# Dense U and V blocks of a group in one transfer each, and sparse phases of 19, 17, 17 and 11 groups

## The reference

```python
# per block of 128 tokens: eb = the 8 x 16 chosen experts of each token, gb = their gates
h = jnp.einsum('td,ted->te', xb, u[eb])          # u, v: (16384, 1024)
a = jax.nn.gelu(h, approximate=False) * gb
y = jnp.einsum('te,ted->td', a, v[eb])
# afterwards: h = layer_norm(alpha * h + y)
```

## Time and profile before

| | |
|---|---|
| median of 3 runs | 3060.47 us (3056.7 to 3060.66) |
| the profiled execution | 3062.79 us |
| its span, first to last instruction | 3061.1 us |
| mean granted TensorE clock | 0.938 |
| TensorE busy | 85% of the span |
| VectorE busy | 75% |
| GpSimd busy | 53% |
| ScalarE busy | 34% |
| moved by DMA | 833 MB |

### The profile page before, as it was taken

The page is one execution under the profiler, slowest core; times in us unless marked ns, Lnnn a source line. Parts: engine busy times, 40 slices in busy tenths (PEclk is TensorE's granted clock), DMA queues, the critical chain, the costliest instruction groups (busy, mean ns, idle before and its releaser), DMA issues.

```text
span 3061.1 us, 40460 instructions
## 1 busy us (share of the span) xinstructions
PE 2617.2 (85%) x14808; PEld 2033.3 (66%) x14808; DVE 2307.9 (75%) x4894; ACT 1049.6 (34%) x1649; POOL 1620.0 (53%) x1187
## 2 busy tenths in 40 slices
PE   7998788889996565644678999999999999999996
PEld 5886676778775565542445767777767777677775
DVE  4512667657999899965777778777778777789999
ACT  4412334333544676751112222322222322222322
POOL 0010011024887555545666666677666767766774
PEclk9999899999998787876889999999999999999999
DMA  4323222131111799999999999999999999999995
GB/s 129 127 81 118 85 87 87 45 119 52 58 59 36 260 300 309 322 296 373 379 383 387 391 386 382 401 394 397 387 394 376 408 404 409 391 382 347 366 377 209
DMA packets 309808, 833.44 MB, mean 272 GB/s; under 512 B 26128, under 2 KB 114640, under 8 KB 309616
## 3 DMA queue, kind: packets, MB, share of 16 engines
q0 software_dynamic: 150864, 548.60, 46.7%
q1 hardware_dynamic: 158752, 282.31, 26.1%
HBM read 771.93 MB, written 58.88 MB: 271 GB/s over the span
## 4 chain that ended last, share of the span: by engine, by line
PE 18%; DVE 12%; DMA 12%; POOL 8%; issue 5%; ACT 0%; SPq 0%; DVEq 0%; ACTq 0%; POOLq 0%
DMA e_u_row<-in_u,ids 11%; POOL hold L2081 5%; DVE e_u_row L2319 3%; PE psum L2157 3%; PE psum L2124 3%; PE psum L2158 3%; PE psum L2159 3%; PE psum L2125 3%; PE psum L2126 2%; PE psum L2172 2%; POOL e_u_row L2072 2%; DVE e_y L2309 2%; DVE e_u_row L2328 1%; DVE e_vl L2277 1%; DVE hold L2328 1%
## 5 line engine op out<-in xcount | busy, mean ns | idle before, releaser
L2072 POOL DMA_INDIRECT e_u_row<-in_u,ids x384 | 485.6, 1265 | 330.3 <-DVE ids L2319 236.3
L2319 DVE CUSTOM_DVE_ANT_0 e_u_row<-e_u_row,hold 128x1024 f32<-128x1024 f32 x384 | 468.3, 1224 | 242.6 <-DMA e_u_row<-in_u,ids 242.0
L2157 PE MATMUL psum<-e_vh,e_ah 128*128 128x512 f32 x1024 | 420.7, 411 | 102.1 <-DVE e_y L2309 82.6
L2081 POOL DMA_INDIRECT hold<-in_v,ids x376 | 435.5, 1158 | 134.4 <-issue 108.8
L2158 PE MATMUL psum<-e_vl,e_ah 128*128 128x512 f32 x1024 | 409.2, 400 | 0.0
L2159 PE MATMUL psum<-e_vh,e_al 128*128 128x512 f32 x1024 | 407.4, 398 | 0.0
L2124 PE MATMUL psum<-x1d,e_uh 128*128 128x512 f32 x864 | 341.0, 395 | 0.0
L2125 PE MATMUL psum<-x1d,e_uh 128*128 128x512 f32 x864 | 337.2, 390 | 0.0
L2157 PEld LDWEIGHTS psum<-e_vh,e_ah 128*128 128x128 f32 x1024 | 198.1, 193 | 209.2 <-DVE e_y L2309 109.9
L2126 PE MATMUL psum<-x1d,e_ul 128*128 128x512 f32 x864 | 336.3, 389 | 0.0
L2309 DVE TENSOR_TENSOR e_y<-e_y,psum 128x512 f32<-128x512 f32 x464 | 299.7, 681 | 13.1 <-PE psum L2159 13.1
(11 more groups left out here) (407 smaller groups left out, 5628.9 us busy)
## 6 DMA issues: line engine op xcount, KB each, us to landing
e_vr<-in_v SPq DMA_DIRECT2D x128, 512.0 KB, 6.7
e_ur<-in_uT SPq DMA_DIRECT2D x108, 512.0 KB, 7.2
s_G<-g_tile SPq DMA_DIRECT2D x8, 4096.0 KB, 27.0
e_g<-s_G SPq DMA_DIRECT2D x64, 512.0 KB, 9.0
ids<-in_w_ch SPq DMA_DIRECT2D x17, 512.0 KB, 4.1
s_ch<-p_out POOLq DMA_DIRECT2D x16, 512.0 KB, 3.3
hold<-in_wq SPq DMA_DIRECT2D x16, 512.0 KB, 4.4
hold<-in_v,ids POOLq DMA_INDIRECT x476, 8.7
```

The costliest lines, as they stand in the source:

```text
L2072: pool.indirect_dma_start(out=u_ring[n % U_RING][:], out_offset=None, in_=io["u"], in_offset=bass.IndirectOffsetOnAxis(ap=id_u[:, s, k:k + ...
L2081: pool.indirect_dma_start(out=v_ring[m % V_RING], out_offset=None, in_=io["v"], in_offset=bass.IndirectOffsetOnAxis(ap=id_v[:, t:t + 1], a ...
L2157: nc.tensor.matmul(acc, ah[s][j][:, r], vh[s][j][:, c], start=(first and j == 0), stop=False)
L2319: nc.vector.tensor_tensor_reduce(row, row, xs[:, s, :], 1.0, 0.0, ALU.mult, ALU.add, hs[:, s, k:k + 1]).then_inc(dotted, 1)
```

## The change

- `PHASE` becomes (0, 19, 36, 53, 64): the first phase has 19 groups, the second 17; the third and the last stay at 17 and 11.
- The arrays in HBM are laid out by groups. `uT` has both blocks of a group side by side in each partition's row, and V has a second copy `v2` in the same manner (the old `v` stays, for the gathers). So both blocks are one transfer of 1 MB whose runs are 8 KB. U blocks loaded singly (before the experts, and the first dense group's) take their 4 KB out of the 8 KB rows (`u_block`).
- The raw V blocks have no tile of their own: `v_raw[s]` is declared and released, so that `v_low[s]` gets its addresses; the subtraction then writes the low part over the raw data. The V load of g waits until TensorE is done with values(g-2), whose low part stands there, and no longer for the splits.
- The U load of g+1 waits for both splits of g.
- ScalarE splits V after both halves of the rest of its list. VectorE's split of V block 0 moves from ahead of weigh 1 to behind the last dot, just ahead of adds 6 and 7.

```diff
--- before.py
+++ after.py
@@ -52,7 +52,7 @@
 U_RING, V_RING, Z_RING = 4, 8, 4
 WIDE, NARROW = 4, 4
 CAND = WIDE * TOPK + (TOPK - WIDE) * NARROW
-PHASE = (0, 18, 36, 53, 64)
+PHASE = (0, 19, 36, 53, 64)
 AHEAD = AHEAD_R + AHEAD_G
 LEVELS = 7
 
@@ -98,6 +98,11 @@
 
 def ts(start, size):
     return bass.ds(start, size)
+
+
+def u_block(io, b):
+
+    return io["uT"][b // 2][:, b % 2]
 
 
 def wait_apart(engine, tick, semaphore, value):
@@ -1266,7 +1271,7 @@
         def sync(sp):
             def load_u(b):
                 sp.wait_ge(u_lo, b)
-                sp.dma_start(ur[:], io["uT"][b]).then_inc(u_in, 16)
+                sp.dma_start(ur[:], u_block(io, b)).then_inc(u_in, 16)
 
             def store_hidden(b):
                 sp.wait_ge(gelu[b % 2], b // 2 + 1)
@@ -1898,7 +1903,7 @@
                 sp.dma_start(xs[:, 0, :], scr["x1"][0:P, :]).then_inc(x_in[0], 16)
                 for b in range(TD // TG):
                     sp.wait_ge(u_lo, b)
-                    sp.dma_start(ur[:], io["uT"][AHEAD_R + b]).then_inc(u_in, 16)
+                    sp.dma_start(ur[:], u_block(io, AHEAD_R + b)).then_inc(u_in, 16)
                     if b == 1:
                         sp.wait_ge(numbered, 1)
                         sp.wait_ge(tr, ND)
@@ -1939,12 +1944,15 @@
         v_ring = [hold[:, NS + n, :] for n in range(V_RING)]
         u_ring = [sb(f"e_u_row{n}", [P, D]) for n in range(U_RING)]
         y = sb("e_y", [P, ND, D])
-        ur = [sb(f"e_ur{j}", [P, KC, P]) for j in range(2)]
-        vr = sb("e_vr", [P, D])
+        u_raw = sb("e_ur", [P, 2, KC, P])
+        ur = [u_raw[:, j] for j in range(2)]
         uh = [sb(f"e_uh{j}", [P, KC, P], F32R) for j in range(2)]
         ul = [sb(f"e_ul{j}", [P, KC, P], F32R) for j in range(2)]
         vh = [[sb(f"e_vh{s}{j}", [P, D], F32R) for j in range(2)] for s in range(2)]
-        vl = [[sb(f"e_vl{s}{j}", [P, D], F32R) for j in range(2)] for s in range(2)]
+        with ExitStack() as below:
+            v_raw = [below.enter_context(nc.sbuf_tensor(f"e_vr{s}", [P, 2, D], F32)) for s in range(2)]
+        v_low = [sb(f"e_vl{s}", [P, 2, D], F32R) for s in range(2)]
+        vl = [[v_low[s][:, j, :] for j in range(2)] for s in range(2)]
         ah = [[sb(f"e_ah{s}{j}", [P, TD], F32R) for j in range(2)] for s in range(2)]
         al = [[sb(f"e_al{s}{j}", [P, TD], F32R) for j in range(2)] for s in range(2)]
         gt = sb("e_g", [P, TD // TG, 2, TG])
@@ -1958,10 +1966,11 @@
         rstd = sb("f_rstd", [P, NT])
         shift = sb("f_shift", [P, NT])
         lng, lnb = (ur[j].rearrange("p k e -> p (k e)") for j in range(2))
-        ln_in = 16 * (NG + 1)
+        ln_in = 16 * (SHORT + 2)
 
         u_in = [sem(f"u_in{j}") for j in range(2)]
-        v_in = [sem(f"v_in{j}") for j in range(2)]
+        pair_in = sem("u_pair_in")
+        v_in = [sem(f"v_in{s}") for s in range(2)]
         g_in = sem("g_in")
         u_hi = [sem(f"u_hi{j}") for j in range(2)]
         u_lo = [sem(f"u_lo{j}") for j in range(2)]
@@ -2018,37 +2027,42 @@
         with nc.Block() as block:
             @block.sync
             def _(sp):
-                def load_u(g, j):
-                    if g < SHORT:
+                def load_activated(g):
+                    for j in range(2):
                         sp.wait_ge(a_mul[j], g)
                         sp.dma_start(ur[j].rearrange("p k e -> p (k e)")[:, 0:TD],
                                      scr["hidden"][2 * g + j]).then_inc(u_in[j], 16)
-                    else:
+
+                def load_first_u():
+                    for j in range(2):
                         sp.wait_ge(a_mul[j], SHORT)
+                        sp.dma_start(ur[j], io["uT"][SHORT][:, j]).then_inc(u_in[j], 16)
+
+                def load_u(g):
+                    for j in range(2):
                         sp.wait_ge(u_lo[j], g - SHORT)
-                        sp.dma_start(ur[j][:], io["uT"][2 * g + j]).then_inc(u_in[j], 16)
+                    sp.dma_start(u_raw[:], io["uT"][g]).then_inc(pair_in, 16)
 
                 def load_gates(g):
                     for j in range(2):
                         sp.wait_ge(a_mul[j], g)
                     sp.dma_start(gt[:], scr["G"][g]).then_inc(g_in, 16)
 
-                def load_v(g, j):
-                    sp.wait_ge(v_lo[1 - j], g + j)
-                    sp.dma_start(vr[:], io["v"][(2 * g + j) * NK:(2 * g + j + 1) * NK, :]).then_inc(v_in[j], 16)
-
-                for j in range(2):
-                    load_u(0, j)
+                def load_v(g):
+                    if g >= 2:
+                        sp.wait_ge(y_mm, Q * (g - 1))
+                    sp.dma_start(v_raw[g % 2][:], io["v2"][g]).then_inc(v_in[g % 2], 16)
+
+                load_activated(0)
                 for g in range(NG):
                     if SHORT < g + 1 < NG:
-                        for j in range(2):
-                            load_u(g + 1, j)
+                        load_u(g + 1)
                     load_gates(g)
-                    load_v(g, 0)
-                    if g + 1 <= SHORT:
-                        for j in range(2):
-                            load_u(g + 1, j)
-                    load_v(g, 1)
+                    load_v(g)
+                    if g + 1 < SHORT:
+                        load_activated(g + 1)
+                    elif g + 1 == SHORT:
+                        load_first_u()
                     if g == 0:
                         for t in range(ND):
                             sp.dma_start(y[:, t, :], scr["x1"][TS + t * P:TS + (t + 1) * P, :]).then_inc(x1_in, 16)
@@ -2195,15 +2209,18 @@
             @block.scalar
             def _(act):
                 def split_u(g, j):
-                    act.wait_ge(u_in[j], 16 * (g + 1))
+                    if g > SHORT:
+                        act.wait_ge(pair_in, 16 * (g - SHORT))
+                    else:
+                        act.wait_ge(u_in[j], 16 * (SHORT + 1))
                     act.wait_ge(h_mm[j], g - SHORT)
                     nc.scalar.activation(uh[j][:], ur[j][:], ACT.Copy).then_inc(u_hi[j], 1)
 
                 def split_v(g, j):
-                    act.wait_ge(v_in[j], 16 * (g + 1))
+                    act.wait_ge(v_in[g % 2], 16 * (g // 2 + 1))
                     if g >= 2:
                         act.wait_ge(y_mm, Q * (g - 1))
-                    nc.scalar.activation(vh[g % 2][j][:], vr[:], ACT.Copy).then_inc(v_hi[j], 1)
+                    nc.scalar.activation(vh[g % 2][j][:], v_raw[g % 2][:, j, :], ACT.Copy).then_inc(v_hi[j], 1)
 
                 def split_a(g, j):
                     act.wait_ge(a_mul[j], g + 1)
@@ -2274,7 +2292,7 @@
 
                 def split_v(g, j):
                     dve.wait_ge(v_hi[j], g + 1)
-                    nc.vector.tensor_tensor(vl[g % 2][j][:], vr[:], vh[g % 2][j][:].bitcast(F32),
+                    nc.vector.tensor_tensor(vl[g % 2][j], v_raw[g % 2][:, j, :], vh[g % 2][j][:].bitcast(F32),
                                             ALU.subtract).then_inc(v_lo[j], 1)
 
                 def weigh(g, j):
@@ -2394,7 +2412,6 @@
                     if SHORT <= g + 1 < NG:
                         split_u(g + 1, 0)
                     dot_rows(g, 3)
-                    split_v(g, 0)
                     weigh(g, 1)
                     dot_rows(g, 4)
                     split_a(g, 1)
@@ -2409,6 +2426,7 @@
                     if g:
                         gather(g - 1, 4, 6)
                     dot_rows(g, 7)
+                    split_v(g, 0)
                     if g:
                         gather(g - 1, 6, Q)
                     split_v(g, 1)
@@ -2568,8 +2586,9 @@
         "a_log": a["gdn_a_log"][0], "dt_bias": a["gdn_dt_bias"][0], "norm_w": a["gdn_norm_w"][0],
         "sinks": sinks, "w_out": w_out, "ln1_g": a["ln1_g"][0], "ln1_b": a["ln1_b"][0],
         "wq": blocks(a["peer_wq"][0]), "keysT": np.ascontiguousarray(keys),
-        "uT": np.ascontiguousarray(a["peer_u"][0].reshape(NK, NK, KC, P).transpose(0, 3, 2, 1)),
-        "u": a["peer_u"][0], "v": a["peer_v"][0], "ln2_g": a["ln2_g"][0], "ln2_b": a["ln2_b"][0],
+        "uT": np.ascontiguousarray(a["peer_u"][0].reshape(NK // 2, 2, NK, KC, P).transpose(0, 4, 1, 3, 2)),
+        "u": a["peer_u"][0], "v": a["peer_v"][0],
+        "v2": np.ascontiguousarray(a["peer_v"][0].reshape(NK // 2, 2, NK, D).transpose(0, 2, 1, 3)), "ln2_g": a["ln2_g"][0], "ln2_b": a["ln2_b"][0],
         "consts": constants(), "wmask": window_masks(),
     }
```

## The result

The changed kernel takes 3073.59 us (median of 7 runs, 3067.94 to 3079.66) against 3060.08 for the kernel before in the same series: ratio 1.0039, 95% interval 1.0027 to 1.0051. It is 13.5 us slower where 10 us faster was forecast, and 1.6 us beyond the range of 3036 to 3072. The profiled execution took 3076.07 us.

The account below looks back on a forecast made before the run. It took DMA to bound groups 0 to 9, TensorE the middle and VectorE the tail. Its terms, led by -10.4 us for fewer rows, summed to -10.1 us, giving 3050.4 us; range 3036 to 3072 for 8 in 10 runs.

Parts of the forecast that it names:

- Nothing but DMA is full: Groups 0 to 9: DMA share 1.00, TensorE 64% and VectorE 69% busy; fewer rows there were to save 10.4 us.
- In the 1,100 us between neither is worth anything: Between first and last 250 us: fewer bytes or a shorter VectorE list gain nothing while DMA keeps up.
- The V pair's 3 us in that stretch: First stretch: V's load no longer waits for VectorE's splits, so gathers are asked for sooner, 3 us saved.
- Phase 1: +4 forecast: Phase 1's 17 groups: more rows a group, 0 to 0.5 us each, 0 to +9, middle +4 us.
- Phase 1 becomes DMA-bound: Rival, chance 0.24: at 389 GB/s phase 1's bytes outlast TensorE, 13 us in place of +4, total 3059.
- 5 us of slack to hide it in: Phases 1 and 2: VectorE, 79% busy, has 5 us a group to hide later U loads and gates.
- Dense loads clump: Rival, chance 0.20: U, gates and V leave together, rows and gates come late; 23 us, total 3073.
- Two thirds of the turns for 8 KB packets: Within a rival: 8 KB packets taking turns with 4 KB ones give the dense queue two thirds of 409 GB/s.
- The prediction's estimate of 234 us: Merging 117 pairs of transfers at 2.0 us fixed each would save 234 us; the prediction said the trace disagrees.
- 8 ns a packet: An 8 KB run for two of 4 KB saves 8 ns if one packet; at most 2.8 us in all.
- The tail: +3 forecast: Last ten groups: gates behind 1 MB of U instead of 0.5 come later, 0 to +10, taken as +3 us.

Follow-up runs that it names:

- phases_only: Only the phases changed to 19, 17, 17, 11 on the kernel before, V and U loaded as before: 3067.09 us, ratio 1.0041.
- ring3_18: The kernel before with three buffers for gathered U rows in place of four, last phase's ring one shorter too: 3307.31 us, ratio 1.0800.
- ring5_18: transfers_only with a fifth buffer for gathered U rows: 3036.22 us, ratio 0.9924 to the kernel before.
- transfers_only: The changed kernel with the old phases of 18, 18, 17, 11: 3074.20 us, ratio 1.0063 to the kernel before.
- v_pair_18: The kernel before with V in one transfer over its low part and V's splits moved, U in two transfers: 3062.13 us, ratio 1.0017.
- u_pair_18: The kernel before with only the U blocks in one transfer of 8 KB runs: 3068.77 us, ratio 1.0035.
- the bare wait: The kernel before with U still in two loads, both waiting for both splits, nothing merged: 3075.27 us, ratio 1.0054.
- runs4k_18: transfers_only with the same merged 1 MB transfers in 4 KB runs from the old layouts: 3076.31 us, ratio 1.0065 to the kernel before.

## Why the prediction was wrong

**"Nothing but DMA is full" in groups 0 to 9: this step failed.** I read share 1.00 and 389 GB/s, against a ceiling of 409, as bound by bytes, and priced 0.82 rows fewer at 10.4 us. They brought 2 us in phases_only and under 1 in the changed kernel, and even that is no gain: the six kernels with four buffers and the old phases take 257.2 to 261.6 us for the stretch (mean 259), the four with the new phases 258.1 to 260.9 (mean 260). The kernel before had holes of its own inside its share of 1.00, here beside full windows of 410:

```profile
1490.00:1495.00 5.00, 4.12 (x18) 3.46 (x19) 5.00 (x9) 0.63 (x1) 4.09 (x4) 1.00 0.82 235
```

What the runs show in its place is the round trip of the U rows through four buffers, at least as much as bytes: a fifth buffer takes 6.0 us from the stretch on the old phases and 13.7 on the new ones, and one fewer adds 50. But a round trip is no fixed time, or fewer rows would have shortened the stretch by the ring theory too. From the issue of a U gather to the next issue into the same buffer it is 13.7 us on average in the kernel before and 14.5 in phases_only (12.3 in `ring3_18`, 16.7 in `ring5_18`). From issue to dot it stays at 10.5 and 10.6; from the dot to the next issue it grows from 3.3 to 3.9. Why, no run shows.

VectorE's 53.2 us of waits for U rows could not tell rows that come late from bytes that run out: over 1390 to 1620 they are 49.2 us before and 54.9 in `ring5_18`, which is faster. GpSimd's waits for a free buffer go with the ring: 72.2 us with three buffers, 43.7 before, 30.9 in `ring5_18`. Only changing the number of buffers tells the two apart.

**"In the 1,100 us between neither is worth anything": this failed too.** Groups 10 to 18 were to gain 2.1 us; they took 4.2 more in phases_only and 1.1 in the changed kernel. And of the 38.1 us that the fifth buffer takes from groups 0 to 52 of transfers_only, 32.1 lie in groups 10 to 52. Phase 2 then takes 434.0 us, 25.5 a group, where I had taken 25.9 for TensorE's own pace because it was 99% busy.

**The V pair's 3 us in that stretch.** The staging tile's waits did end, but TensorE now waited 20.9 us for the low part of V there, 12.4 before:

```profile
DVE e_u_row L2337 <- DMA e_u_row<-in_u,ids: 55.2, 14, 9.7
...
PE psum L2171 <- DVE e_vl L2295: 20.9, 6, 7.1
```

The wait changed its place: V's load now waits for TensorE's own progress, and the split of block 0 stands behind the last dot in VectorE's list. Which of the two it was is not shown. The V pair alone costs 0.17% over the whole kernel. Whether 3 us came in this stretch can't be read: `v_pair_18` takes 257.3 us for it, and so does `u_pair_18` (257.2), where V is as before.

**Phase 1: +4 forecast, +12.4 measured.** The rival "Phase 1 becomes DMA-bound" had the place and, at 13, the price, but its reason is only a part. In the chain that ended last, over 1900 to 2320, the landings of U rows hold 15.3% in the kernel before and 29.4% in the changed one. The fifth buffer takes back 10.6 us of the stretch with the same bytes (454.3 to 443.7). But it takes 10.1 from transfers_only too, which has the old phases, so what it gives back is mostly the loss of the merged transfers. The phases themselves cost 4.1 us there on merged transfers with four buffers and 3.6 with five, about what I had charged for bytes. Why they cost 6.7 on the kernel before, and why phase 1 has most of the loss, is not shown; that phases and U pair both take slack from the same ring would fit.

**The U pair: "5 us of slack to hide it in".** This step failed too. I had put its cost in phases 1 and 2 at nothing. VectorE's 79% was an average; while the row at the head of its list hasn't landed, as in 1590 to 1600, what stands behind it waits too. The U pair cost 0.35% on the old phases and the bare wait 0.54%, half of that outside the tail. The rival "Dense loads clump" named this with 0.3 us a group and gave it 0.20. Its total, 3073, is what was measured, but partly by luck: its 10 us in the tail did not come, and groups 19 to 52 lost 16 where it had 13 for all 43 groups before the tail.

**Two thirds of the turns for 8 KB packets.** The large share is there, but not for that reason. Counted over the packets of the traces, from 2 to 4 us behind each issue of a U pair between 1700 and 2740, the hardware queue has 0.80 of the bytes in the changed kernel and 0.79 in `runs4k_18`, whose runs are 4 KB; in the kernel before, behind a first half, it is 0.54. Whether the pair takes that share or fewer gathers are under way then, no run shows. The Trainium skill ("DMA: Bandwidth & Descriptors", "Queues, rings and completion order") counts a turn in whole packets, there typically 9 to 17 descriptors each; the step from that to one 8 KB run against one of 4 KB was the prediction's own, and `runs4k_18` speaks against this step and doesn't test the page's rule. The prediction's estimate of 234 us was worked out from the fit that the Trainium skill gives under "Anatomy of one DMA" (same page) for transfers issued from GpSimd, while SP issues the merged loads; merging alone cost 17 us.

**8 ns a packet: about right, and worth nothing.** 277,792 of 292,959 packets under 8 KB leave 15,167 of that size or more; before there were 192 (309,808 less 309,616), so 14,975 are new, as 53 U and 64 V transfers of 128 promise (14,976). In 2370 to 2752 the hardware queue took 24.9% of 16 engines for 37.70 MB, 40.4 us of engine time a MB, for 41.0 before:

```profile
q1 hardware_dynamic: 6176, 37.70, 24.9%
```

1.5% less, near the 2% that 8 ns would give; the shares are rounded to 0.1%, so this is no closer than that. In the time it shows nowhere: the same transfers in runs of 4 KB took as long.

**The tail: +3 forecast, about -1 measured.** With U merged and the split in its old place (`u_pair_18`) VectorE waits 4.9 us for gates there, in the changed kernel 0.8: the move of split_v covered the later gates.

Still open: the parts don't add up. Phases alone 0.41% and transfers alone 0.63% would make 1.0%, and the change measured 0.39%, in a series of its own on other runs. The intervals, some 0.15% each, don't close that gap, and I haven't tried to. On merged transfers the phases cost nothing by the medians (3074.20 and 3073.59, in different series), on the kernel before 10 us. Nor is it shown what GpSimd's changed list is worth apart from the fifth buffer, what the buffer would give without the merged V loads, which make the room for it, or whether a sixth would give more.

## What to carry to other kernels

A DMA share of 1.00 with a rate 5% under the best slice was no plain byte limit here: look for windows of 5 us where the share drops, and ask what the ring of buffers in flight allows. Where an engine works through an ordered list fed by a shallow ring, don't count on its average slack: a load that is merged, and so leaves with the later of its halves, cost 0.35% with four buffers and nothing with five. Freed memory may be worth more than the change that freed it: the merged transfers had made the kernel 17 us slower than before, and the 4 KB that they freed, as a fifth buffer, made it 22 us faster than before.

## What the runs showed of the hardware

A window's share of 1.00 can hold holes: full windows of 5 us in the kernel before show 1.03, and 1390 to 1640 comes to 1.00 with 1490 to 1495 at 0.82 and 235 GB/s in it. Granted clock followed the stalls: it was 0.50, the lower of its two levels (1.2 GHz), in 1595 to 1605 of the changed kernel, where TensorE did nothing from 1592 to 1603. The next 12 matmuls of 512 columns started 0.43 us apart for the most part, and those after them, with the clock back at 1.00, 0.23 us apart, so a round trip that stalls TensorE is paid again in its next matmuls. Over 1390 to 1620 the clock averages 0.77 with three buffers, 0.80 in the kernel before and 0.84 with five.
